# Layer 0's FFN conditioning pairs: which engine's queue loads them

## The reference, cut to what matters

```
def adaln(c, w, b):
    return jnp.split(jax.nn.silu(c) @ w + b, 6, axis=-1)

def modulate(x, g, shift, scale):
    return rms_norm(x, g) * (1.0 + scale[:, None, :]) + shift[:, None, :]

def swiglu_sublayer(x, shift, scale, gate, g, w_gate, w_up, w_down):
    h = modulate(x, g, shift, scale)
    return x + gate[:, None, :] * ((jax.nn.silu(h @ w_gate) * (h @ w_up)) @ w_down)
```

## Time and profile before

| | |
|---|---|
| median of 3 runs | 2760.37 us (2759.95 to 2762.34) |
| the profiled execution | 2757.93 us |
| its span | 2756.2 us |
| PE busy | 2676.4 us, 97% |
| DVE busy, ACT busy | 1426.5 us, 1160.5 us |
| PE waiting for a pair in `aring` at line 1090, whole kernel | 2.6 us |
| DMAs of the ring (line 622), each | 1024 KB, 6.9 us to landing |

### The profile page before, as it was taken

How to read it: one execution, slowest core, us unless ns; L and a number is a source line. 1 busy time by engine, 2 the same in 40 slices (tenths; PEclk the granted TensorE clock), 3 DMA queues, 4 the chain that set the end, 5 groups by cost and what they waited for, 6 DMA issues and landing times.

```text
span 2756.2 us, 48520 instructions
## 1 busy us (share of the span) xinstructions
PE 2676.4 (97%) x20155; PEld 2473.9 (90%) x20155; DVE 1426.5 (52%) x1983; ACT 1160.5 (42%) x1521; POOL 95.9 (3%) x136
## 2 busy tenths in 40 slices
PE   5899999999999999999999999998999999999998
PEld 1688988888898888989999899898999999999998
DVE  1588967664444333444444556656445444445444
ACT  2433256453433322434443446535444433444433
POOL 1100011100000000000000000001000000000000
PEclk8999999999999999999999999999999999999999
DMA  9977769777777788776465544344544455445453
GB/s 392 370 286 275 288 231 179 295 281 284 272 290 260 292 318 317 281 282 244 160 237 161 163 153 136 110 134 159 168 162 161 147 160 190 158 164 167 143 161 128
DMA packets 110042, 603.61 MB, mean 219 GB/s; under 512 B 24829, under 2 KB 26301, under 8 KB 53578
## 3 DMA queue, kind: packets, MB, share of 16 engines
q1 hardware_dynamic: 109898, 601.56, 62.3%
HBM read 592.02 MB, written 9.49 MB: 218 GB/s over the span
## 4 chain that ended last, share of the span: by engine, by line
PE 91%; DMA 4%; DVE 2%; ACT 2%; issue 1%; SPq 0%; DVEq 0%; ACTq 0%
PE ps L882 27%; PE ps L884 26%; PE ps L883 26%; PE ps L1090 5%; DMA pre_ring<-in_w_ada 3%; DMA aring<-in_w_ada 1%; PE ps L1248 1%; ACT w_hi L1409 1%; PE ps L1249 1%; PE ps L1250 1%; PE ps L1103 1%; DMA raw<-in_w_dn 1%; DVE w_lo L1882 1%; PE ps L1072 0%; PE ps L1058 0%
## 5 line engine op out<-in xcount | busy, mean ns | idle before, releaser
L1882 DVE TENSOR_TENSOR w_lo<-raw,w_hi 128x2048 fp32r<-128x2048 f32 (+2 forms) x410 | 804.5, 1963 | 1024.7 <-ACT w_hi L1409 1024.6
L882 PE MATMUL ps<-act_hi,w_hi 128*128 128x288 f32 x4128 | 1234.1, 299 | 6.5 <-DVE w_lo L1882 4.6
L883 PE MATMUL ps<-act_hi,w_lo 128*128 128x288 f32 x4128 | 1219.7, 295 | 0.0
L884 PE MATMUL ps<-act_lo,w_hi 128*128 128x288 f32 x4128 | 1215.5, 294 | 0.0
L1409 ACT ACTIVATE w_hi<-raw 128x2048 fp32r<-128x2048 f32 (+2 forms) x410 | 673.9, 1644 | 1050.3 <-PE ps L884 1033.2
L882 PEld LDWEIGHTS ps<-act_hi,w_hi 128*128 128x128 f32 x4128 | 775.6, 188 | 58.6 <-issue 55.6
L884 PEld LDWEIGHTS ps<-act_lo,w_hi 128*128 128x128 f32 x4128 | 779.0, 189 | 0.0
L883 PEld LDWEIGHTS ps<-act_hi,w_lo 128*128 128x128 f32 x4128 | 777.1, 188 | 0.0
L882 PE MATMUL ps<-hid_hi,w_hi 128*128 128x288 f32 x1408 | 418.8, 297 | 0.6 <-DVE w_lo L1882 0.6
L883 PE MATMUL ps<-hid_hi,w_lo 128*128 128x288 f32 x1408 | 415.4, 295 | 0.0
L884 PE MATMUL ps<-hid_lo,w_hi 128*128 128x288 f32 x1408 | 414.0, 294 | 0.0
(11 more groups left out here) (339 smaller groups left out, 1757.6 us busy)
## 6 DMA issues: line engine op xcount, KB each, us to landing
raw<-in_w_gu SPq DMA_DIRECT2D x172, 1024.0 KB, 5.2
aring<-in_w_ada SPq DMA_DIRECT2D x166, 1024.0 KB, 6.9
raw<-in_w_dn SPq DMA_DIRECT2D x128, 704.0 KB, 4.1
raw<-in_w_ab SPq DMA_DIRECT2D x40, 1024.0 KB, 6.5
raw<-in_w_out SPq DMA_DIRECT2D x64, 512.0 KB, 4.7
raw<-in_w_cd SPq DMA_DIRECT2D x26, 1024.0 KB, 5.2
pre_ring<-in_w_ada SPq DMA_DIRECT2D x16, 1024.0 KB, 10.1
side<-in_w_ada SPq DMA_DIRECT2D x6, 1024.0 KB, 9.8
```

Of the source, the lines that this page charges most:

```text
L882: pe.matmul(bank, w_hi[:, h, cols], hi[:, kt, :], start=begin, stop=False)
L883: pe.matmul(bank, w_lo[:, h, cols], hi[:, kt, :], start=False, stop=False)
L884: mm = pe.matmul(bank, w_hi[:, h, cols], lo[:, kt, :], start=False, stop=end)
L1882: dve.tensor_tensor(w_lo[:, h, 0:w], raw[:, par, h * KT * P:h * KT * P + w], w_hi[:, h, 0:w].bitcast(F32), ALU.subtract).then_inc(split_do ...
```

## The change

ACT issues the loads of pairs 27 to 76 (`ACT_PAIRS`), and SP skips these. ACT issues pair p+1 in the step whose visit is of pair p, right after its copy of h0 of the next step, and it waits there for the same two `ada_used` counts that SP waited for. At the restart step the place is behind `split_behind_restart`. Pair 26 and the pairs outside the range stay with SP. The weights stay with SP.

```
+ACT_PAIRS = range(27, 77)
...
                         for p in (pair_at_end(seg, ls - 1), pair_of(seg, ls)):
-                            if p is not None:
+                            if p is not None and p not in ACT_PAIRS:
                                 load_pair(p)
...
+            def load_pair(p):
+
+                for r in range(2):
+                    rows = t["w_ada"][(DOUBLES[p // 4] + r) * 4 + p % 4]
+                    act.wait_ge(ada_used, 4 * PRE + 2 * (p - 1) + 1 + r)
+                    act.dma_start(aring[:, r, :], rows).then_inc(ada_landed[r], 16)
...
                     elif nxt and not (nxt is OUT0 and end):
                         split(nxt, n + 1, 1 - par, 0)
+                    if pair_of(seg, ls) is not None and pair_of(seg, ls) + 1 in ACT_PAIRS:
+                        load_pair(pair_of(seg, ls) + 1)
```

## The result

The changed kernel takes 2771.97 us in the median of 6 runs (2766.48 to 2775.19), the kernel before 2761.36 us (2759.13 to 2763.26) measured beside it. The ratio is 1.0038 with a 95% interval of 1.0027 to 1.0049: 10.6 us slower. The forecast was 2777.1 us, 16.7 us slower, with a range of 2761.5 to 2787.

A forecast was written before the change was run, and what follows sets the result against it. PE was taken to bound every step, busy 97% of the span. Stalls of 12.65 us in down steps and 4.04 at the restart made 16.7 us, on 2760.37 giving 2777.1 us; range 2761.5 to 2787.

The forecast's parts named there:

- What decides: Down steps: visits stand 10.85 us apart, leaving a pair 8.96 us from issue to next visit; gu steps have room.
- Taking pairs off SP gains nothing: Removing 50 pairs' issues and waits from SP: worth 0, because SP waits 537.3 us for DVE's `w_lo` anyway.
- ACT's issues, steady steps: 100 issues on ACT, 0.4 us each, fit a 5.07 us hole behind its copy of h0 in down steps: cost 0.
- fourth rival (slow issue): Each issue on ACT takes 1183 ns, sending second blocks 0.78 us later: 27.6 us slower in all, 2788.0 us; chance 0.06.
- h0 gets in between: Down steps: the weights' first half moves on its own queue amid the pair's bytes, 1.65 us per pair, stalls 12.65; chance 0.50.
- five quick ones without a turn or gu weights: Down pairs landing after 7.0 us, no turn of a double in the step: slack 1.42, stall 0.23 each, 1.2 together.
- late one with gu weights: Down pair landing after about 8.2 us, with gu weights (2.40 us) issued behind it: stall 2.2 us.
- late one with a turn: Down pair landing after 8.5 us; a turn of a double gives PE 0.80 us more work: slack 0.72, stall 0.9.
- Pair 27: Restart step: ACT issues only after its `split_behind_restart` copy, 1.64 us stall, plus 2.40 for gu weights behind it: 4.0 us.
- The pair stays ahead of h0: DMA engines finish what was queued first; only the restart step's late issue costs, 1.64 us: 2762.0 us; chance 0.19.
- h1 gets in as well: Down steps and restart: late pairs also share engines with the weights' second half: 24.2 us slower, 2784.6 us; chance 0.17.
- Not slower: Down steps: a queue of their own lands pairs within 7.0 us, removing today's 1.0 us stall: 2759.4 us; chance 0.08.

## Why the prediction was right, and where its sizes were off

**What decides.** The prediction named the down steps, where a pair has 8.96 us. Shown: they alone lose 11.0 us by the medians (only the down pairs by ACT), and the rest 1.5, within the error (all but the down pairs).

**Taking pairs off SP gains nothing.** Right. SP's waits for visits turned into waits for `w_lo`, 763.2 us where they were 537.3, and in none of the three stretches was PE idle for less time than before.

**ACT's issues, steady steps: 0.** Right. Two issues took 0.82 to 1.42 us on ACT (0.80 to 1.55 on SP before), in ACT's hole behind the copy of h0. The second block went out 0.37 to 0.43 us behind the first, and one queue with ACT as issuer ran as fast as before. The fourth rival (slow issue) is out.

**h0 gets in between: 12.65 us in all, 1.65 us for each pair in down.** Right in kind and in the price of a pair, too large in the sum. The waits rose from 1.0 to 10.7 us, 9.7 instead of 12.65, and 11 visits waited instead of 13. The 6.9 and 7.9 us of landing are medians over first and second blocks together. A visit waits for the second block, and that one landed 1.58 us later in the mean of the 15 pairs, taken pair by pair (0.9 to 2.6). So h0 joins 3.4 us late and still moves nearly all of its bytes before the pair's end. The h0 of 928.47 shows it: it landed after 8.2 us, at 936.7, and the pair beside it at 927.57 + 9.44 = 937.01.

```profile
DMA to landing us min/median/max: 8.2/8.2/8.2
```

The sum came out too large because I gave every pair the same rise. The first three pairs of the stretch went from 8.2, 7.2 and 9.44 us to 9.44, 8.98 and 10.30: 1.2, 1.8 and 0.9 more. The quick pairs (7.0 us before) rose more than the late ones (8.0 to 8.5), and much of that went into their slack. The five quick ones without a turn or gu weights waited 0 to 0.53 us (0.23 forecast), the four late ones 0.88 to 1.52 (1.43), the one that stalled already 0.87 more (1.65), the late one with gu weights 1.31 (2.2), the late one with a turn 0.27 (0.9).

A visit that waits also brings h0 closer to the next pair. In the kernel after they go out 1.28 us apart without a wait, and 0.71 us apart behind the visit of 948.58, since the split that releases h0 is not held up by the visit. What that does to the landing is not shown: the pair behind the visit of 948.58 lands only after 10.30 us, but it is the one that took 9.44 before. Here are the four issues, on ACT's and then on SP's timeline:

```profile
927.19 0.82 ACTq L1527 DMA_DIRECT2D aring<-in_w_ada  x2
...
950.53 1.29 ACTq L1527 DMA_DIRECT2D aring<-in_w_ada  x2
```

```profile
928.47 0.33 SPq L604 DMA_DIRECT2D raw<-in_w_dn  x1
...
951.24 0.33 SPq L604 DMA_DIRECT2D raw<-in_w_dn  x1
```

The Trainium skill's rule that the prediction weighed ("DMA: Bandwidth & Descriptors", "Queues, rings and completion order") is borne out in the shares once both queues move, 41 packets to 39. That the weights join in at once, as the prediction read it, is not: they joined after 3.3 and 3.4 us.

**Pair 27: 4.0 us.** This is the term that was mis-sized: it measured 1.3. I let ACT issue when its copy ends, and it issued when the copy started, 1.26 us earlier (601.71 instead of 602.97). The prediction had that as the lower bound, 1.27 us less. And I let all 2.40 us of h0 in; with that delay the second block (issued 0.43 us behind the first) landed after 7.89 us, only 0.9 more than the 7.0 that I took for it alone.

**The rivals.** "The pair stays ahead of h0" is out by the shares and by h0 cut to 64 KB. "h1 gets in as well" is out as a cost of its own by the same run, though h1 does have its part once h0 has made a pair late; that part was not measured. "Not slower" is out by the result, and today's slow landings are not due to weights ahead on SP's queue: with h0 cut to 64 KB the pair issued at 1024.87, with one fetch on q8 in its time, still landed after 8.5 us, and the next one, with none, after 7.2. That speaks for late pairs with a fetch; the latest of before (9.44 us) has none in its time, and its cause stays open. Of the 6.1 us by which the forecast of the change was too large (16.7 against 10.6), pair 27 is 2.7 and the down steps 3.0 (12.65 forecast, 9.7 measured).

## What to carry to other kernels

A single queue is also an order: with pair and weights on one queue, whichever engine issued them, the pair that was issued first was not held up by the weights behind it (1.0 and 1.8 us of waits in down, against 10.7 on two queues). Before moving one of two streams to another engine's queue, take the tighter stream's window, subtract its landing, and see whether the other stream's bytes fit into what is left; the issuing engine's time is the smaller question. And delaying the looser stream is no cure if it then meets the next transfer's start.

## What the runs showed of the hardware that was not expected

A transfer issued on a second queue while the first queue's transfer was under way moved no bytes for 3.3 us (h0 at 871.40, beside a pair of 2 MB), 3.4 us (h0 at 928.47, the same) and 2.8 us (a pair at 959.99, beside the two halves, 1.4 MB, with the halves held back). After that, in the first two cases, the two queues moved about as many packets each; in the third the halves were nearly done. ACT issued a DMA at 601.71 while its own copy from 601.70 to 602.97 was running: an issue that stands behind an ACTIVATE in ACT's program didn't wait for its end.
